# A token mixer's scan on one core: inverse in 64x64 blocks, values times inverse made at once, scores in other banks, two attention blocks in every step, part of the out-projection in the drain

## The reference, cut to what matters

```python
o_a = swa_sink_attention(qa, ka, va, swa_sinks, slopes_swa)   # 4 heads of 64, window 128
o_b = moba_attention(qb, kb, vb, slopes_moba)                 # 4 heads of 64, causal over 512
o_c = gated_delta_rule(qc, kc, vc, g, beta)                   # 4 heads of 128, chunks of 64
mixed = jnp.concatenate([o_a, o_b, rms_norm_2(o_c, dn_norm) * jax.nn.silu(z_c)], axis=-1)
return mixed @ w_out
```

```python
L = jnp.where(strict, einsum('bhnid,bhnjd->bhnij', k_beta, k) * decay, 0.0)
sol = triangular_solve(L + eye(C), concatenate([v * beta, k_beta * exp(g)]))
u, w = sol[..., :dv], sol[..., dv:]
def step(state, xs):
    v_new = u_c - w_c @ state
    o = qd_c @ state + a_c @ v_new
    state = state * exp(gl_c) + kd_c.T @ v_new
    return state, o
```

## Time and profile before

| what | value |
|---|---|
| runs | 2301.5, 2303.11, 2301.55 us; median 2301.55 us |
| profiled execution | 2295.11 us, span 2293.3 us, mean granted clock 0.988 |
| TensorE busy | 2222.1 us, 97% of the span |
| VectorE, ScalarE, GpSimd busy | 1138.2, 918.2, 1070.9 us |
| inverse, levels 1 to 5 | 1685.46 to 1735.56 us of the span |
| out-projection, first three tiles | 1832.97 to 1850.59 us |

### The profile page before, as it was taken

One profiled execution on the slowest core, in us unless ns is written; L12 is line 12 of the kernel. 1 busy time (PEld: TensorE's weight loads), 2 busy tenths in 40 slices (PEclk: granted clock), 3 DMA queues, 4 the chain that ended last, 5 costly groups with the idle time before them and its releaser, 6 DMA issues.

```text
span 2293.3 us, 32123 instructions
## 1 busy us (share of the span) xinstructions
PE 2222.1 (97%) x10384; PEld 1796.2 (78%) x10384; DVE 1138.2 (50%) x1529; ACT 918.2 (40%) x1597; POOL 1070.9 (47%) x789
## 2 busy tenths in 40 slices
PE   8999999999999999999999999999999888999996
PEld 6788888888888887777787788878798666778885
DVE  7842234444432453555328523357584347888613
ACT  4243344434433444444332444343635444333322
POOL 5654444454454444444446544444312333555553
PEclk9999999999999999999999999999999899999998
DMA  3232322222223222111122322232100021222332
GB/s 136 92 110 91 101 92 98 95 99 93 101 92 101 97 92 83 57 64 56 65 83 92 101 100 95 98 106 90 67 28 1 1 73 56 91 91 95 106 101 100
DMA packets 53643, 194.46 MB, mean 85 GB/s; under 512 B 6080, under 2 KB 6336, under 8 KB 53568
## 3 DMA queue, kind: packets, MB, share of 16 engines
q1 hardware_dynamic: 52560, 191.13, 25.0%
q10 hardware_dynamic: 1008, 2.33, 0.3%
HBM read 191.34 MB, written 2.10 MB: 84 GB/s over the span
## 4 chain that ended last, share of the span: by engine, by line
PE 49%; issue 30%; POOL 17%; DVE 2%; ACT 1%; POOLq 1%; ACTq 0%; DVEq 0%
POOL w_lo L594 17%; PE proj L665 11%; PE proj L667 11%; PE proj L666 11%; PE aux L799 2%; PE proj L824 1%; PE proj L916 1%; PE aux L916 1%; PE proj L753 1%; PE proj L755 1%; PE proj L754 1%; PE aux L802 1%; PE aux L810 1%; PE proj L1018 0%; PE aux L1006 0%
## 5 line engine op out<-in xcount | busy, mean ns | idle before, releaser
L594 POOL TENSOR_TENSOR w_lo<-w_stage,w_hi 128x512 fp32r<-128x512 f32 x716 | 994.0, 1397 | 1021.4 <-ACT w_hi L1213 1020.6
L1213 ACT ACTIVATE w_hi<-w_stage 128x512 fp32r<-128x512 f32 x716 | 438.1, 627 | 781.9 <-PE proj L667 708.5
L665 PE MATMUL proj<-xh,w_hi 128*128 128x512 f32 x1696 | 670.6, 395 | 12.5 <-POOL w_lo L594 12.5
L666 PE MATMUL proj<-xl,w_hi 128*128 128x512 f32 x1696 | 661.5, 390 | 0.0
L667 PE MATMUL proj<-xh,w_lo 128*128 128x512 f32 x1696 | 661.3, 390 | 0.0
L665 PEld LDWEIGHTS proj<-xh,w_hi 128*128 128x128 f32 x1696 | 319.0, 188 | 95.9 <-POOL w_lo L594 26.4
L667 PEld LDWEIGHTS proj<-xh,w_lo 128*128 128x128 f32 x1696 | 319.1, 188 | 67.4
L666 PEld LDWEIGHTS proj<-xl,w_hi 128*128 128x128 f32 x1696 | 319.2, 188 | 66.9 <-issue 2.4
L665 PE MATMUL proj<-act_h,w_hi 128*128 128x512 f32 (+1 forms) x840 | 327.1, 389 | 0.6 <-POOL w_lo L594 0.6
L667 PE MATMUL proj<-act_h,w_lo 128*128 128x512 f32 (+1 forms) x840 | 326.8, 389 | 0.0
L666 PE MATMUL proj<-act_l,w_hi 128*128 128x512 f32 (+1 forms) x840 | 326.8, 389 | 0.0
(11 more groups left out here) (316 smaller groups left out, 2416.0 us busy)
## 6 DMA issues: line engine op xcount, KB each, us to landing
w_stage<-stream SPq DMA_DIRECT2D x358, 512.0 KB, 3.3
out<-x_res SPq DMA_DIRECT2D x4, 512.0 KB, 2.6
x_res<-x SPq DMA_DIRECT2D x2, 512.0 KB, 8.4
consts_sb<-consts ACTq DMA_DIRECT2D x1, 832.0 KB, 4.5
x_res<-x ACTq DMA_DIRECT2D x1, 512.0 KB, 7.4
x_res<-x SPq DMA_DIRECT2D x1, 256.0 KB, 3.5
x_res<-x ACTq DMA_DIRECT2D x1, 256.0 KB, 5.3
pos_i<-pos ACTq DMA_DIRECT2D x1, 256.0 KB, 2.7
```

The lines of the kernel that those rows point to most:

```text
L594: pool.tensor_tensor(w_lo[:, at, :], w_stage[:, at, :], w_hi[:, at, :].bitcast(F32), ALU.subtract).then_inc(stage_free, 1)
L665: pe.matmul(o, w_hi[:, slot, cols], hi, start=(b == 0), stop=False)
L666: pe.matmul(o, w_hi[:, slot, cols], lo, start=False, stop=False)
L1213: act.activation(w_hi[:, u % RING, :], w_stage[:, u % RING, :], ACT.Copy).then_inc(hi_done, 1)
```

## The change

The inverse and the products before it work on the 64x64 chunks alone: each product of a 128x128 block becomes two products of 64x64, on the upper left and the lower right quarter of the array (`per_chunk`), and VectorE and ScalarE handle 256 elements per partition where they had 512. Spreading the gates for "bg" becomes two products of 256 columns, each giving 64 partitions. The transpose of `xt` becomes products with an identity. "wt" becomes two halves of 64 contracted rows, "wh" and "wt", two heads in turn. The inverse times the scaled values, for all chunks, is made once, "u", after the inverse; VectorE copies it ("uc"), and in a step it adds it to the product with the state, in place of ScalarE's copy "vn". The first step is folded into this beginning. The scores go to `proj`, the values, outputs and updates to `aux`. Steps 1 to 7 take two softmax blocks each; none are left after them. VectorE does the two maxima of a step after the new values, and the scale of the first block after the state's update. The output sums move to the even steps. The last block is scaled by VectorE. Three of the eight k-steps of the out-projection's first three tiles stand in the drain.

```diff
 CHUNKS = S // CHUNK
-PAIRS = 16
-SLOTS = ((0, 1), (2, 3), (4, 5), (6, 7), (8, 9), (10, 11), (12,), (13,))
-AFTER_STEPS = (14, 15)
+PAIRS = 2 * CHUNKS
+EARLY_OUT = 3
+SPARE_BANK = 0
...
+        def compact(ap):
+            return ap[:, 0:4 * CHUNK].rearrange("p (b k) -> p b k", k=CHUNK)
...
-            return aux[:, 2 * (k % 2):2 * (k % 2) + 2, 0:pair_of(k)[3]]
+            return proj[:, 2 * (k % 2):2 * (k % 2) + 2, 0:pair_of(k)[3]]
...
+        def norm_bank(h):
+            return proj[:, SPARE_BANK, :] if h == 1 else aux[:, h, :]
+        def update_bank(h):
+            return proj[:, 2 + h, :] if h < 2 else aux[:, h - 2, :]
...
+            def per_chunk(h, b, stationary, moving):
+                for blk in range(4):
+                    for r in (0, CHUNK):
+                        mm = pe.matmul(compact(head_bank(h, b))[r:r + CHUNK, blk, :], stationary(blk, r), moving(blk, r),
+                                       start=True, stop=True)
+                return mm
...
-                    made(spread_row(h, 0, 32 + h), ("bg", h))
+                    for r in (0, CHUNK):
+                        at = CONSTS["ident"] + 32 + h
+                        mm = pe.matmul(compact(head_bank(h, 0))[r:r + CHUNK, :, :],
+                                       consts[0:64, at:at + 1].broadcast_to([64, CHUNK]),
+                                       rows[0:64, :].rearrange("p (b r k) -> p b r k", r=2, k=CHUNK)[:, :, r // CHUNK, :],
+                                       start=True, stop=True)
...
-                    made(per_block(h, 0, lambda blk: kf[:, h, blk * P:blk * P + P],
-                                   lambda blk: kb[:, h, blk * P:blk * P + P]), ("g1", h))
+                    made(per_chunk(h, 0, tokens_of(kf, h), tokens_of(kb, h)), ("g1", h))
...
-                    made(per_block(h, 0, None, lambda blk: xt[:, h, blk, :], turn=True), ("x1", h))
+                    made(per_chunk(h, 0, chunk_of(xt, h), ident_of), ("x1", h))
...
-                        made(per_block(h, 1, lambda blk: e_mat[:, h, blk, :], lambda blk: x_mat[:, h, blk, :]), (f"y{l}", h))
+                        made(per_chunk(h, 1, chunk_of(e_mat, h), chunk_of(x_mat, h)), (f"y{l}", h))
...
-                        mm = per_block(h, 0, lambda blk: y_mat[:, h, blk, :], lambda blk: xt[:, h, blk, :])
+                        mm = per_chunk(h, 0, chunk_of(y_mat, h), chunk_of(xt, h))
                         if l < LEVELS - 1:
-                            mm = per_block(h, 1, lambda blk: xt[:, h, blk, :], lambda blk: y_mat[:, h, blk, :])
+                            mm = per_chunk(h, 1, chunk_of(xt, h), chunk_of(y_mat, h))
                         made(mm, (f"p{l}", h))
-                for h in HEADS:
-                    pe.wait_ge(mix_dve, DVE_STEP[f"xt{LEVELS - 1}", h])
-                    made(per_block(h, 0, lambda blk: blocks_of(vf[:, h, :])[:, blk, :],
-                                   lambda blk: xt[:, h, blk, :]), ("wt", h))
+                attend(0)
+                for half in range(2):
+                    for first in (0, 2):
+                        pair = ((first, CHUNK * half), (first + 1, CHUNK - CHUNK * half))
+                        for h, r in pair:
+                            if half:
+                                pe.wait_ge(mix_pe, PE_STEP["wh", first + 1])
+                            else:
+                                pe.wait_ge(mix_dve, DVE_STEP[f"xt{LEVELS - 1}", h])
+                        for blk in range(4):
+                            for h, r in pair:
+                                mm = pe.matmul(head_bank(h, 0)[:, blk * P + r:blk * P + r + CHUNK],
+                                               blocks_of(vf[:, h, :])[r:r + CHUNK, blk, :], xt[r:r + CHUNK, h, blk, :],
+                                               start=True, stop=True)
+                                if blk == 3:
+                                    made(mm, ("wt" if half else "wh", h))
+                for h in HEADS:
+                    if h >= 2:
+                        pe.wait_ge(mix_act, ACT_STEP["nw", h - 2])
+                    for blk in range(4):
+                        for r in (0, CHUNK):
+                            mm = pe.matmul(update_bank(h)[r:r + CHUNK, blk * P:blk * P + P], xt[r:r + CHUNK, h, blk, :],
+                                           vbeta[r:r + CHUNK, h, blk, :], start=True, stop=True)
+                    made(mm, ("u", h))
...
+                if k == 1:
+                    pe.wait_ge(mix_dve, DVE_STEP["uc", 1])
...
+                pe.wait_ge(mix_dve, DVE_STEP["st", c - 1])
+                for h in HEADS:
+                    mm = pe.matmul(aux[r:r + CHUNK, 0, h * P:h * P + P], vf[:, h, toks], state[:, h, :],
+                                   start=(h == 0), stop=True, skip_group_check=True)
...
+                    pe.wait_ge(mix_dve, DVE_STEP["vn", c])
+                else:
+                    pe.wait_ge(mix_dve, DVE_STEP["uc", 3])
+                def values_of(h):
+                    return vnew[r:r + CHUNK, h * P:h * P + P] if c else vbeta[0:CHUNK, h, 0, :]
+                for h in HEADS:
+                    mm = pe.matmul(aux[:, 1, h * CHUNK:h * CHUNK + CHUNK], values_of(h), within_of(h)[r:r + CHUNK, blk, :],
                                    start=(c == 0 and h == 0), stop=True, skip_group_check=True)
...
+                attend(1)
+                turn_values_in(0)
+                turn_values_in(1)
+                output_and_update(0, -1)
+                turn_values_in(2)
+                turn_values_in(3)
+                for c in range(1, CHUNKS):
+                    a, b = 2 * c, 2 * c + 1
                     attend(a)
                     new_values(c)
-                    if b > a:
-                        attend(b)
-                    if a == 2:
-                        pe.wait_ge(mix_act, ACT_STEP["avc", 3])
+                    attend(b)
                     turn(a - 2)
                     output_and_update(c, a - 4)
                     values(a - 3, c)
-                    if b > a:
-                        turn(b - 2)
-                    if c % 2:
-                        output_sums(c // 2, a - 3)
-                    if b > a:
-                        values(b - 3, c)
-                for k in AFTER_STEPS:
-                    attend(k)
-                    turn(k - 2)
-                    values(k - 3, CHUNKS - 1)
+                    turn(b - 2)
+                    if c % 2 == 0:
+                        output_sums(c // 2 - 1, a - 3)
+                    values(b - 3, c)
+                output_sums(CHUNKS // 2 - 1, PAIRS - 4)
+                pe.wait_ge(mix_act, ACT_STEP["ex", PAIRS - 1])
+                assert (tile.n + TOGETHER) % BANKS == SPARE_BANK
+                pe.wait_ge(taken, tile.now(TOGETHER))
+                out_products(0)
                 turn(PAIRS - 2)
+                out_products(1)
                 pe.wait_ge(mix_act, ACT_STEP["osqrt"])
                 values(PAIRS - 3, CHUNKS - 1)
+                turn(PAIRS - 1)
                 pe.wait_ge(mix_dve, DVE_STEP["orc"])
...
                 made(mm, "ornt")
-                turn(PAIRS - 1)
+                out_products(2)
                 values(PAIRS - 2, CHUNKS - 1)
                 pe.wait_ge(mix_dve, DVE_STEP["orn"])
-                for h in HEADS:
-                    made(pe.matmul(banks(4 + h), consts[0:4, CONSTS["ident"] + h:CONSTS["ident"] + h + 1]
-                                   .broadcast_to([4, P]), rn[0:4, :], start=True, stop=True), ("ob", h))
+                norm_rows(0)
+                norm_rows(1)
                 values(PAIRS - 1, CHUNKS - 1)
-                pe.wait_ge(mix_act, ACT_STEP["mc", PAIRS - 1])
+                norm_rows(2)
+                norm_rows(3)
+                for k in range(EARLY_OUT, DT):
+                    out_products(k)
+                tile.up(TOGETHER)
+                pe.wait_ge(mix_dve, DVE_STEP["on", 1])
+                for t in range(DT - TOGETHER):
+                    products(tile.n % BANKS, DT, of_mixed)
+                al.up(DT)
+            def norm_rows(h):
+                made(pe.matmul(norm_bank(h), consts[0:4, CONSTS["ident"] + h:CONSTS["ident"] + h + 1]
+                               .broadcast_to([4, P]), rn[0:4, :], start=True, stop=True), ("ob", h))
+            def out_products(k):
+                pe.wait_ge(al_done, al.n + k + 1)
...
-                    together(of_mixed, lambda k: pe.wait_ge(al_done, al.n + k + 1), DT)
-                    for t in range(DT - TOGETHER):
-                        products(tile.n % BANKS, DT, of_mixed)
-                    al.up(DT)
...
+                maxima(0)
+                for h in HEADS:
+                    dve.wait_ge(mix_pe, PE_STEP["u", h])
+                    made(dve.tensor_copy(vbeta[:, h, :, :], blocks_of(update_bank(h))), ("uc", h))
+                maxima(1)
+                update_state(0)
+                scale_of(0)
+                scaled_x(0)
```

(54 more changed lines are left out.)

249 lines of the change are left out of this document (110 added, 139 removed).

## The result

The changed kernel takes 2263.74 us (median of four runs, 2259.54 to 2264.93), the kernel before 2301.53 in the same comparison: a ratio of 0.9841, 95% interval 0.9825 to 0.9856. That is 37.8 us less, where 42.1 were forecast. The profiled execution took 2259.54 us with a span of 2257.2; before it was 2295.11 with 2293.3. The two spans are 36.1 us apart, and the medians of a later comparison 35.7 (2297.42 and 2261.76), so the gain is known to some 2 us.

A forecast was written before the change was run, and what follows sets the result against it. TensorE, busy 97% of the span, was taken as the bound, with idle and slow stretches in the tail. Terms -1.6 - 3.2 - 24.1 + 0.4 - 1.4 - 12.2 = -42.1 us took 2301.55 to 2259 us; range 2247 to 2292.

The forecast's parts named there:

- Parts 1 and 2: Products ahead of the inverse: "bg" on two column halves, -1.6 us; "g1" and "g2" as 64 short records each, -3.2 us together.
- Part 4: The inverse: 896 quarter records at 28 ns, 26.0 us with the ramp for 50.1, -24.1 us (bounds 0 and -25).
- rival A: 64x64 products don't overlap, as they write one bank from two row halves: 56 ns a record, 2290 us; 18%.
- Part 5: Beginning of the scan, with "u" made there: 13.6 us for 13.16, +0.4 us (bounds -1 and +4).
- Part 6: Steps 1 to 6 of the scan: "nv" halved, second block in step 6, longer waits; -1.4 us (bounds -5 and +6).
- Part 7: Step 7, drain and first three out-projection tiles: early k-steps hide waits and clock loss; 35.0 us for 47.2, -12.2 us.
- part 3: "x1" ahead of the inverse: 16 one-record transposes become 64 records, 1.8 us for about 1.8, so 0; "bg2" stays.
- the +2.6 in part 6: Work added to steps 1 to 6: step 6 takes a second softmax block and step 7 begins with wider scores; +2.6 us.
- B: Quarter products overlap only in part, as TensorE can't start records so fast: at 40 ns a record 2271 us; 14%.
- C: The scan becomes a chain through VectorE and ScalarE: 2 us more in each of six steps, 2271 us; 9%.
- D: The clock goes to 1.2 GHz where four quarters replace full products, from "g1" to step 0: 2313 us; 5%.

## Why the prediction was right

- **Parts 1 and 2.** From their start to the next record "bg" took 1.87 us for 3.63, "g1" and "g2" 2.02 each for 3.49: 1.8 and 2.9, where 1.6 and 3.2 were forecast. The stage lost 4.4 of the forecast 4.8, since the in-projection's last record ahead of "g1", "g2" and "x1" now takes 0.3 us to the group's first one, where it took 0.2. (The stage is the same 37.35 us in the second profile of the changed kernel.)
- **Part 4, more than half of the gain.** 29.1 ns a record for 28. The 28 was chosen from two indirect rows (both kinds of halves overlap) with a bound of 56 on the other side, and one quarter alone did measure 58.5. Part 4 came out 0.8 us short, mostly by this 1 ns a record. The inference that VectorE would be late at once was not borne out: it has 22.8 us of work in 26.8, and doubled products were paid in full.
- The bank, which rival A rested on: all these products write one bank from two row halves, and they overlap. The Trainium skill, page "TensorEngine Tiling (Array Packing)", section "Restrictions and Gotchas", says that different row tiles cannot access the same bank at the same time. The measurement differs: these quarters are different row tiles and write one bank, on different partitions of it, at 29.1 ns a record against 58.5 alone. What the rule means for tiles that write the same partitions no run here shows.
- **Part 5.** 1.1 us better than forecast; no wait is left in it (busy 12.44 of 12.44), where I had put 1.0 us.
- **Part 6.** Steps 1 to 6 were to lose 1.4 us at an unchanged clock loss of 3.3 us. They have 54.82 us, with a loss of 0.09 x 54.82 = 4.9. Take out the clock and it is 51.4 before, 49.9 after: -1.5, so the work and the waits were right and the clock's loss, left at 3.3, was 1.6 us short. The waits come to 3.3 us for the forecast 3.8: 0.47 in step 2 (0.4), 0.74 in step 3 (1.3), 1.29 in step 5 (1.3), none in steps 4 and 6 (0.4 each), 0.81 in step 1, where none was forecast.
- **Part 7, the term that was mis-sized.** The forecast was 31.5 us of work, 3.5 of waits and nothing for the clock. Measured: 38.90 = 32.1 + 1.75 + 0.13 x 38.90, which is 5.1. Work was right, waits half. To strike out all 12.1 us because they are "no work" was wrong for the clock's 6.8 of them: only 1.7 went. The sign that the prediction gave for itself, a clock near 1.00 in the drain, was missed (0.87), while the wait of 2.8 us did go.
- **The sum.** 42.1 us had 35.3 of work and waits and 6.8 of clock. At full clock the runs measured 2267 before and 2231 to 2232 after, 35 to 36 us; the clock's share stayed, at a mean of 0.987 and 0.986. Stage by stage the forecast promised 5.4 us too much: 3.9 in part 7, 1.6 in part 6, 0.8 in part 4 and 0.4 in parts 1 and 2, less 1.1 in part 5 and 0.2 in part 3. The prediction was right in its mechanisms, and out by one thing in the main, the clock in parts 6 and 7. That the medians came within 4.3 us of it is in part the luck of one comparison; by those of the later one it is 6.4.
- Two sums of the prediction don't come out as written. The items of the +2.6 in part 6 add up to 2.5. The low end of the range, 2247, is said to be parts 1, 6 and 7 halfway to their better bounds; that gives 2256, and the whole way 2253.
- Rivals B, C and D did not occur: 29.1 ns; waits of 0.55 us a step (3.32/6), not 2; the inverse at a granted clock of 1.00.

## What to carry to other kernels

Where a block-diagonal matrix is multiplied as full tiles, products of its blocks on opposite quarters of the array need twice the records at about a quarter of the time each, so half the time; a run with all records on one quarter shows how much of that is overlap. When a stage's granted clock is below 1.00, write its length as work, waits and clock loss, and don't book the clock's part as gain unless something is named that raises it. Compare two versions at an equal mean clock before believing a few microseconds: here 0.001 of clock is worth 2.3 us (0.001 x 2260), more than any of the moves on ScalarE and VectorE brought.

## What the runs showed of the hardware

- Two opposite quarters writing the same bank, on different partitions, work beside each other: 29.1 ns a record together, 58.5 alone, 111.8 for the full array. Starts in the changed kernel alternate with 36 and 22 ns, and records added there cost 27.6 ns.
- Products on different quarters don't start in program order: with each group's upper quarter issued ahead of its lower one, products of the next group started ahead of the last of the group before (1687.67 and 1687.72 us), and the inverse took 36.8 ns a record, where all records on one quarter took 58.5.
- The half clock (1.2 GHz) falls in different places in executions of the same code. After a wait of 2.0 us at the same group the next eight records took 3.67 us in one execution and 5.37 in another, and shared code ahead of the change took 1628.21 and 1633.25 us in these two.
- With the three k-steps of 512 column products taken out of the drain, the drain and first tiles had a granted clock of 0.78, where the changed kernel had 0.87 in both of its profiles. Whether TensorE's waits bring the clock down was not settled here: the added transposes left 4.4 us of idle time where there had been 5.1 and 7.0.
